# Dot products that read h from PSUM in the steps in which its banks are free

## The reference

```python
def peer_block(h, w_pq, sub_keys, expert_u, expert_v):
    ...
    s = jnp.einsum('nhpc,hpkc->nhpk', q, sub_keys.astype(F32))
    s_top, i_top = lax.top_k(s, PEER_TOPK)
    ...
    e = i1 * PEER_N_KEYS + i2
    gate = jax.nn.softmax(sc, axis=-1)
    act = jax.nn.gelu(jnp.einsum('nd,nhkd->nhk', h.astype(F32), expert_u[e].astype(F32)), approximate=False)
    return jnp.einsum('nhk,nhkd->nd', gate * act, expert_v[e].astype(F32))
```

## Time and profile before

| what | value |
|---|---|
| median of the runs | 4193.62 us |
| profiled execution: span from first to last instruction | 4435.8 us |
| profiled execution: any other time of its own | none given |
| TensorE, VectorE, ScalarE, GpSimd busy | 2995.1, 2799.8, 917.6, 2465.2 us |
| gathers of `stream` | 2 x 1024, mean 1163 and 1111 ns |
| dot products | 1024, mean 1223 ns |
| data moved by DMA | 1388.96 MB, mean 313 GB/s |

### The profile page before, as it was taken

How to read it: one execution, slowest core, us unless ns; L and a number is a source line. 1 busy time by engine, 2 the same in 40 slices (tenths; PEclk the granted TensorE clock), 3 DMA queues, 4 the chain that set the end, 5 groups by cost and what they waited for, 6 DMA issues and landing times.

```text
span 4435.8 us, 41900 instructions
## 1 busy us (share of the span) xinstructions
PE 2995.1 (68%) x12168; PEld 1491.0 (34%) x12168; DVE 2799.8 (63%) x6694; ACT 917.6 (21%) x2005; POOL 2465.2 (56%) x2288
## 2 busy tenths in 40 slices
PE   5968877976866777866677778885666654444435
PEld 3546545645414433422223334441222221010001
DVE  6576851324665466668766766666776668657662
ACT  1423110233411244421111134331111110000000
POOL 1010110102576565676777777667777767777775
PEclk8988988966687877877888888767878877777777
DMA  6575983336699888899999999889999999999998
GB/s 234 182 310 218 386 328 104 106 126 215 230 360 348 313 312 285 306 345 359 370 378 386 362 358 354 326 309 332 380 376 375 382 357 338 354 362 360 348 342 310
DMA packets 422338, 1388.96 MB, mean 313 GB/s; under 512 B 46374, under 2 KB 124454, under 8 KB 409822
## 3 DMA queue, kind: packets, MB, share of 16 engines
q0 software_dynamic: 306432, 1216.48, 73.2%
q1 hardware_dynamic: 89390, 140.65, 9.4%
q10 hardware_dynamic: 26288, 29.15, 1.9%
HBM read 1333.57 MB, written 56.86 MB: 313 GB/s over the span
## 4 chain that ended last, share of the span: by engine, by line
POOL 35%; PE 15%; issue 15%; DMA 5%; DVE 4%; another core or an unknown queue 4%; DVEq 1%; ACT 0%; ACTq 0%; SPq 0%; PEldq 0%; POOLq 0%; PEld 0%
POOL st_rows L1525 35%; DMA st_rows<-in_peer_v,st_expert_v 4%; PE st_ps_q L1794 3%; PE st_ps_m L1804 3%; PE st_ps_q L1833 2%; PE st_ps_y L1878 2%; PE st_ps_t L1777 2%; DVE st_rows L2113 1%; PE st_ps_m L1810 1%; DMA st_rows<-in_peer_u,st_expert 1%; PE st_ps_m L1746 1%; PE st_ps_q L1797 1%; PE st_ps_s L1862 1%; DMA st_h<-scr_h 0%
## 5 line engine op out<-in xcount | busy, mean ns | idle before, releaser
L1878 PE MATMUL st_ps_y<-st_rows,st_diag 128*32 128x512 f32 x4096 | 1095.6, 658 | 730.7 <-DMA st_rows<-in_peer_v,st_expert_v 633.1
L1525 POOL DMA_INDIRECT st_rows<-in_peer_u,st_expert x1024 | 1191.3, 1163 | 645.4 <-issue 292.3
L2113 DVE CUSTOM_DVE_ANT_0 st_rows<-st_rows,st_h 128x1024 f32<-128x1024 f32 x1024 | 1218.1, 1223 | 394.4 <-DMA st_rows<-in_peer_u,st_expert 318.5
L1525 POOL DMA_INDIRECT st_rows<-in_peer_v,st_expert_v x1024 | 1137.5, 1111 | 509.6 <-issue 287.9
L1878 PEld LDWEIGHTS st_ps_y<-st_rows,st_diag 128*32 128x32 f32 x4096 | 199.9, 115 | 1585.9 <-issue 957.0
L602 PE MATMUL pd_ps<-pd_w,pd_xnT 128*128 128x256 f32 x1152 | 275.0, 399 | 24.8 <-ACT pd_stage L511 13.7
L1833 PE MATMUL st_ps_q<-st_shared 128*128 128x128 f32 (+3 forms) x1024 | 255.3, 412 | 8.4 <-issue 7.7
L424 POOL DMA_INDIRECT pd_kv<-in_cache_v,pd_rows x32 | 34.4, 1074 | 393.6 <-DVE pd_z L863 378.7
L602 PEld LDWEIGHTS pd_ps<-pd_w,pd_xnT 128*128 128x128 f32 x1152 | 227.8, 201 | 69.8 <-issue 37.3
L1862 PE MATMUL st_ps_s<-st_both,st_pick_tokens 128*128 128x32 f32 (+1 forms) x520 | 88.8, 322 | 213.6 <-issue 194.9
L2153 DVE TENSOR_TENSOR st_shared<-st_shared,st_ps_m 128x256 f32<-128x256 f32 (+5 forms) x176 | 73.2, 416 | 245.4 <-PE st_ps_m L1804 211.2
(11 more groups left out here) (326 smaller groups left out, 3878.4 us busy)
## 6 DMA issues: line engine op xcount, KB each, us to landing
st_shared<-in_w_pq_heads SPq DMA_DIRECT2D x32, 1024.0 KB
st_rows<-in_peer_u,st_expert POOLq DMA_INDIRECT x1024
st_rows<-in_peer_v,st_expert_v POOLq DMA_INDIRECT x1024
pd_w<-in_w_in SPq DMA_DIRECT2D x14, 1024.0 KB
scr_proj<-pd_stage ACTq DMA_DIRECT2D x8, 1152.0 KB
hs_step<-scr_factors SPq DMA_DIRECT2D x20, 416.0 KB
scr_score<-st_sc_out ACTq DMA_DIRECT2D x64, 130.0 KB
st_sc<-scr_score SPq DMA_DIRECT2D x64, 130.0 KB
```

The costliest lines, as they stand in the source:

```text
L1525: pool.indirect_dma_start(rows[n % R][:, :], None, src, bass.IndirectOffsetOnAxis(ap=idx, axis=0)).then_inc(row_loaded[n % R], 16)
L1878: ins = nc.tensor.matmul(ps_y[j * QUAD:(j + 1) * QUAD, c * 512:(c + 1) * 512], diag[k % 2][:, QS * j + q, :], rows[n % R][:, c * 512:(c + ...
L2113: nc.vector.tensor_tensor_reduce(out=rows[n % R][:, :], in0=rows[n % R][:, :], in1=hb, scale=1.0, scalar=0.0, op0=ALU.mult, op1=ALU.add, a ...
```

## The change

In the free steps the dots take h from `ps_m` and not from `h[b % 2]`. ScalarE copies h there, in two halves of 512 columns, before the first free step of a run of free steps and before each free step that begins a block: `H_COPY` is steps 3, 6, 15, 19, 24, 37, 41, 48 and 56. The copy for step `k + 1` stands behind the Gelu of step `k`, and where step `k` is a mixing step behind the exponential for step `k + 2`. It waits for the load of h, for the dots before it, and for the last readers of the banks. TensorE waits for the dots of the last free step before attention or mixing writes the banks again. VectorE waits for the copy. In the other 27 steps the dots read `h[b % 2]` as before.

```diff
+    FREE = [k not in ATTEND and k not in MIX for k in range(STEPS)]
+    H_COPY = [k for k in range(STEPS) if FREE[k] and (k % H == 0 or not FREE[k - 1])]
+    copies_upto = lambda k: sum(c <= k for c in H_COPY)
+    mixes_before = lambda k: 1 + sum(x < k for x in MIX)
+    tiles_before = lambda k: TILE0[1] + sum(0 <= t < len(TILES[g]) for x in ATTEND if x < k for g, t in ATTEND[x])
+    last_free = lambda k: max((x for x in range(k) if FREE[x]), default=-1)
...
+            def copy_h(k):
+
+                b = k // H
+                act.wait_ge(h_loaded[b % 2], 16 * (b // 2 + 1))
+                act.wait_ge(dots_ready, k)
+                act.wait_ge(mix_read, mixes_before(k))
+                act.wait_ge(x_ready, tiles_before(k))
+                for n in range(2):
+                    nc.scalar.copy(ps_m[:, n * 512:(n + 1) * 512], h[b % 2][:, n * 512:(n + 1) * 512])
+                act.drain().then_inc(h_copied, 1)
...
                 weights(k)
+                if k + 1 in H_COPY and k not in MIX:
+                    copy_h(k + 1)
                 if k + 2 < STEPS:
                     exps(k + 2)
+                if k + 1 in H_COPY and k in MIX:
+                    copy_h(k + 1)
...
                 if b > 0:
                     pe.wait_ge(mix_read, b)
+                    free = last_free(next(x for x in MIX if MIX[x] == b))
+                    if free >= 0:
+                        pe.wait_ge(dots_ready, free + 1)
...
                     if mixed["n"] > 0:
                         pe.wait_ge(mix_read, mixed["n"])
+                    free = last_free(min((x for x in ATTEND if ATTEND[x][0] == (g, t)), default=0))
+                    if free >= 0:
+                        pe.wait_ge(dots_ready, free + 1)
...
                 if k % H == 0:
                     dve.wait_ge(h_loaded[b % 2], 16 * (b // 2 + 1))
+                if FREE[k]:
+                    dve.wait_ge(h_copied, copies_upto(k))
                 slots = ATTEND.get(k, ())
                 for s in range(K):
-                    dot(row_u(k, s), h[b % 2][:, :], act_in[k % 2][:, s:s + 1])
+                    dot(row_u(k, s), ps_m[:, :] if FREE[k] else h[b % 2][:, :], act_in[k % 2][:, s:s + 1])
```

More of the change, by code:

```diff
@@ L1316, in stream @@
         score_stored = [sem(f"score_stored{hd}") for hd in range(H)]
+        h_copied = sem("h_copied")
         h_stored, h_loaded, h_used = sem("h_stored"), [sem(f"h_loaded{j}") for j in range(2)], sem("h_used")
```

## The result

The changed kernel takes 4136.1 us (median of 4 runs, 4124.9 to 4137.2) against 4194.1 us before: a ratio of 0.986, 95% interval 0.984 to 0.9885. The forecast was 4073 us (0.971). So it is faster and inside the range, but the gain is 58 us where 121 were forecast.

What follows compares the result with a forecast made beforehand. GpSimd writing gathers, slowed under dots with two SBUF inputs, paced the 64 steps, DMA engines close behind. Of 226 us at most, 107 in four stretches plus 21 elsewhere, 128 us (2.9%), would go: 4073 us, range 3990 to 4175.

Steps and rivals of the forecast that it cites:

- Rivals 3 and 4: 3: gathers stay slow under PSUM dots, 4190 us, chance 0.07; 4: dots read PSUM slowly, 4418 us, chance 0.06.
- rival 5: DMA engines already at their limit for random 4 KB rows; first two stretches give nothing, 4170 us; chance 0.05.
- the four stretches: Steps 20 to 27, 42 to 48, 50 to 55 and 57 to 62: 27 free steps, gather excess 163 us.
- the 386 to 409 given: DMA rate in GB/s limiting free steps after the change; 398 taken, bounds giving 83 and 155 us gain.
- (a): GpSimd itself as next limit: 32 gathers at 1.242 us plus 2.8 us of waits, at least 42.6 us a step.
- Against the median: Step carrying 128 us of the 4435.8 us profiled span, 2.9%, over to the 4193.6 us median, giving 4073.
- the forecast had 107: Gain in the four stretches at 398 GB/s: 20.5, 21.7, 32.3 and 32.1 us, of 163 us excess.
- the 21 counted for ten of them: Gain in us in the other ten free steps, 334 gathers counted at half the stretches' rate.
- Rival 2: Timed runs lack the long GpSimd waits; score steps gain nothing, some 19 others 3.5 us each, 4125 us; chance 0.22.
- the own range of the sum: Range of the forecast case alone, 4030 to 4125 us; this case had chance 0.50.

Runs made afterwards that it cites:

- e2: The change's copies and waits added to the kernel before, but every dot still reads h from SBUF: 4446.8 us, ratio 0.996, on a 4470 chip.
- e7: The full change with gathers that fetch only half of each row (half the data left out): 3965.2 us on a 4190 chip.
- e12: The full change, with only the first sixteenth fetched of 30 later 1 MB key projection loads: 4088.9 us, ratio 0.974.
- e11: The change with dots from PSUM only in the 19 free steps without score matmuls: 4138.9 us, ratio 0.986, on a 4190 chip.
- e9: The kernel before, unedited, profiled again on a 4190 chip: 4197.4 us, ratio 1.001.
- e10: The change with dots from PSUM only in the 18 free score steps: 4189.9 us, ratio 0.998, on a 4190 chip.
- e13: The whole change, unedited, run again on a 4470 chip: 4551.5 us, ratio 1.014 to before.
- e18: The whole change, unedited, run again on another 4470 chip: 4570.8 us, ratio 1.022 to before.
- e1: The kernel before, unedited, profiled again on a 4470 chip: 4449.5 us, ratio 0.997.
- e4: The change with dots from PSUM only in the 19 free steps without score matmuls: 4410.7 us, ratio 0.987, on a 4470 chip.
- e14: The whole change plus 15 short scratch-tile sets with drains on GpSimd in each free step: 4925.4 us, ratio 1.098, on a 4470 chip.
- e3: The change with dots from PSUM only in the 18 free score steps: 4603.0 us, ratio 1.030, on a 4470 chip.
- e6: The kernel before with gathers that fetch only half of each row (half the data left out): 4214.8 us, ratio 1.005, on a 4190 chip.
- e5: The whole change, unedited, run again on a 4190 chip: 4117.3 us, ratio 0.982 to before.

## Why the prediction was right in its sign and wrong in its size

**Right: what costs nothing.** Copies and waits (e2), the dot from PSUM at 1218 ns, no wait of a dot on ScalarE. Rivals 3 and 4 are out, and so is rival 5, which allowed 23 us.

**Right: the DMA engines are late next,** at 407 to 409 GB/s in three of the four stretches, inside the 386 to 409 given. e7 and e12 show it from both sides. The Trainium skill's 358 GB/s (SBUF — State Buffer, the bandwidth table) is passed by 50. In steps 50 to 55 the rate is only 387, at the same share of 1.02; why isn't shown. Where the score steps ahead are left as they were (e11) these steps take 259.7 us at 397 GB/s, not 266.2. The bound by (a), 42.6 us a step, did not hold: steps 57 to 62 take 41.5 us each, since the 2.8 us of waits in it belong to a 4470 chip.

**Wrong: "Against the median", and with it the start of the sum.** The step said "I carry shares over", from an execution of 4436 us to runs of 4194. But the 239 us between the two spans (4435.8 and e9's 4196.7) are not spread like the work: none lies in the first 1016 us, and 75 lie in the four stretches that the sum was made of (1315.3 against 1240.1), part of them in the waits for late releases of row buffers. It started from 377, 373, 354 and 353 GB/s; the kernel as timed was at 398, 404, 375 and 366. By the same rule with e9's rows the four stretches give, at the forecast's 398 GB/s, nothing in the score steps and 275.0 x 23/398 + 276.9 x 32/398 = 15.9 + 22.3 = 38 us, where the forecast had 107; at 409 GB/s they give 367.8 x 11/409 + 320.4 x 5/409 + 275.0 x 34/409 + 276.9 x 43/409 = 9.9 + 3.9 + 22.9 + 29.1 = 66, where it had 130. Measured, e9 to after: 3.0 + 5.1 + 8.8 + 27.9 = 44.8. Steps 57 to 62 gave 27.9 of the 32.1 forecast, the score steps had next to nothing to give (20.5 and 21.7 forecast), and steps 50 to 55 gave a quarter of 32.3.

**The rest of the account.** The remaining steps gave 33.5 us, more than the 21 counted for ten of them, and the attention steps 28 to 36 took 13.9 back: 44.8 + 33.5 - 13.9 - 2.1 ahead of the first gather = 62.3, the difference of the spans. In those attention steps TensorE is busy 383.15 us at a granted clock of 0.72 instead of 367.94 at 0.76, for the same matmuls. It comes with faster score steps ahead of them (e10: 447.5 us at 0.74; e11, without: 440.0 at 0.76), but was not tried by itself, so its cause is open.

**Rival 2 was the right one,** in its numbers (nothing in the score steps, 3.5 us in 19 others, 4125 us) and in its premise that the timed runs lack the long waits. It had 0.22, since the missing 242 us were laid to the profiler as well; the chip was not thought of. The measured 4136.1 us is outside the own range of the sum (4030 to 4125) and inside the stated one only because that took in rival 5 up to 4175. And the sign hung on the chip: on a 4470 chip the change loses (e13, e18), for a reason that no rival had.

**What stays open.** Why three chips deliver these updates late, and whether a drain behind gathers is shorter on the others. The kernel before, too, is 278 us longer on e1's chip than on e9's, 63 of them in steps 28 to 36, where TensorE is busy 406.24 us at a granted clock of 0.66 against 367.94 at 0.76; whether that is a cause or goes with the rest isn't shown. Of the versions tried, PSUM dots in the 19 free steps without score matmuls win on both kinds, 1.3% (e4) and 1.4% (e11); the whole change wins up to 1.8% on one and loses up to 2.2% on the other.

## What to carry to other kernels

Before a share of a profile is carried over to timed runs, ask where the time lies that the two differ by: 239 us that only one of them has change the sum more than any rate in it. When an engine that issues transfers is made faster, first work out the bytes of a stretch over its length, in the execution that is timed; what is left up to the best rate seen, about 410 GB/s here, bounds what such a change can bring. And a slow issuer can be a throttle that something else depends on (e13, e18), so measure on more than one chip.

## What the hardware showed that was not expected

- Five chips in two kinds, 6.5% apart with this kernel (4191 and 4196 against 4465 to 4479 us), the same to 5 us ahead of the first gather (table), and apart only in the steps with gathers. Whether it is the chip or the time that makes the kind isn't told apart.
- 408 GB/s, nine tenths of it random rows of 4 KB, held over 365 us (the first window of after).
- A drain of 5.8 to 8.0 us behind gathers that the profile shows as ended (e14), and a copy on ScalarE that starts 16.8 us after the matmuls that it waits for, seen on 4470 chips alone and with quick gathers alone (e3, e13).
- Half the bytes a row don't make a gather cheaper for GpSimd: a median of 0.949 us beside no VectorE work in e6, 0.941 in e5.
